# Moving the second direction's chain one step ahead and its products one step back in the heads of a hybrid encoder layer

## The reference, cut to what matters

```python
kf, gf = gates(z_fwd, lb_fwd)
kb, gb = gates(z_bwd, lb_bwd)
o_f = _gla_scan(q, kf, v, gf)
rev = lambda a: jnp.flip(a, axis=1)
o_b = rev(_gla_scan(rev(q), rev(kb), rev(v), rev(gb)))
return o_f + o_b
...
b = jnp.cumsum(gb, axis=-2)
o_inter = jnp.einsum('bhtk,bhkv->bhtv', qb * jnp.exp(b), state)
diff = b[:, :, :, None, :] - b[:, :, None, :, :]
decay = jnp.exp(jnp.where(tri[:, :, None], diff, NEG))
att = jnp.einsum('bhtk,bhsk,bhtsk->bhts', qb, kb, decay)
o_intra = jnp.einsum('bhts,bhsv->bhtv', att, vb)
```

## Time and profile before

| | us |
|---|---|
| median of 3 runs | 1864.23 (1863.73 to 1864.8) |
| profiled execution | 1865.62 |
| its span | 1863.9 |
| TensorE busy | 1803.9 (97% of the span) |
| DVE busy | 1193.5 (64%) |
| ACT busy | 835.3 (45%) |
| GpSimd busy | 197.1 (11%) |
| mean granted TensorE clock | 0.985 |

### The profile page before, as it was taken

How to read it: one execution, slowest core, us unless ns; L and a number is a source line. 1 busy time by engine, 2 the same in 40 slices (tenths; PEclk the granted TensorE clock), 3 DMA queues, 4 the chain that set the end, 5 groups by cost and what they waited for, 6 DMA issues and landing times.

```text
span 1863.9 us, 24074 instructions
## 1 busy us (share of the span) xinstructions
PE 1803.9 (97%) x9337; PEld 1551.5 (83%) x9337; DVE 1193.5 (64%) x1408; ACT 835.3 (45%) x1133; POOL 197.1 (11%) x205
## 2 busy tenths in 40 slices
PE   6999999999999999999999999999999999999998
PEld 5899999888778787878787887878888888888887
DVE  6977776788577778686877767776444432244332
ACT  7444444443556556474747464645322232234221
POOL 4000000000130304040302112220000000000000
PEclk9999999999999999999999999999999999999999
DMA  7343444675523232323233231324545535565332
GB/s 227 92 122 114 149 132 141 198 259 163 161 71 108 84 97 88 102 85 89 82 99 91 74 112 55 110 78 153 174 137 152 157 131 163 167 240 180 127 131 75
DMA packets 287661, 240.89 MB, mean 129 GB/s; under 512 B 9657, under 2 KB 233944, under 8 KB 286032
## 3 DMA queue, kind: packets, MB, share of 16 engines
q1 hardware_dynamic: 284096, 227.59, 39.8%
q0 software_dynamic: 3472, 12.05, 1.8%
HBM read 210.80 MB, written 28.80 MB: 129 GB/s over the span
## 4 chain that ended last, share of the span: by engine, by line
PE 76%; DVE 12%; ACT 7%; issue 3%; DMA 1%; SPq 0%; ACTq 0%; DVEq 0%
PE mm_ps L1869 8%; PE mm_ps L1871 8%; PE mm_ps L1870 8%; PE mm_ps L2094 5%; PE mm_ps L2095 5%; PE mm_ps L2093 5%; DVE dif L1476 3%; PE ax_ps L1938 2%; PE ax_ps L1856 2%; PE ax_ps L1858 2%; PE ax_ps L1857 2%; PE ax_ps L1871 2%; PE ax_ps L1870 2%; PE ax_ps L1869 2%; PE ax_ps L2095 2%
## 5 line engine op out<-in xcount | busy, mean ns | idle before, releaser
L343 DVE TENSOR_TENSOR w_lo<-w_raw,w_hi 128x1024 fp32r<-128x1024 f32 (+1 forms) x200 | 271.6, 1365 | 382.5 <-ACT w_hi L334 382.3
L334 ACT ACTIVATE w_hi<-w_raw 128x1024 fp32r<-128x1024 f32 (+1 forms) x200 | 226.8, 1138 | 427.4 <-PE ax_ps L2095 208.5
L1869 PE MATMUL mm_ps<-act_hl,w_hi 128*128 128x512 f32 x960 | 384.6, 401 | 1.3 <-DVE w_lo L343 1.3
L1871 PE MATMUL mm_ps<-act_hl,w_lo 128*128 128x512 f32 x960 | 374.7, 390 | 0.0
L1870 PE MATMUL mm_ps<-act_hl,w_hi 128*128 128x512 f32 x960 | 374.3, 390 | 0.0
L1871 PEld LDWEIGHTS mm_ps<-act_hl,w_lo 128*128 128x128 f32 x960 | 180.1, 188 | 38.9
L1869 PEld LDWEIGHTS mm_ps<-act_hl,w_hi 128*128 128x128 f32 x960 | 180.6, 188 | 36.8 <-issue 1.7
L1870 PEld LDWEIGHTS mm_ps<-act_hl,w_hi 128*128 128x128 f32 x960 | 180.6, 188 | 35.3
L962 ACT ACTIVATE q_hi<-q_raw 128x1024 fp32r<-128x1024 f32 x84 | 87.6, 1057 | 141.7 <-DVE q_raw L1319 81.2
L2093 PE MATMUL mm_ps<-w_hi,act_hl 128*128 128x512 f32 x384 | 149.9, 390 | 0.0
L2095 PE MATMUL mm_ps<-w_lo,act_hl 128*128 128x512 f32 x384 | 149.4, 389 | 0.0
(11 more groups left out here) (299 smaller groups left out, 3818.5 us busy)
## 6 DMA issues: line engine op xcount, KB each, us to landing
w_raw<-in_w_in SPq DMA_DIRECT2D x120, 512.0 KB, 3.8
q_raw<-in_w_in SPq DMA_DIRECT2D x56, 512.0 KB, 5.8
r_in<-in_w_in SPq DMA_DIRECT2D x56, 512.0 KB, 4.7
w_raw<-in_w_ple_gate SPq DMA_DIRECT2D x20, 768.0 KB, 4.4
w_raw<-in_w_out SPq DMA_DIRECT2D x16, 768.0 KB, 4.3
w_raw<-in_w_branch_a SPq DMA_DIRECT2D x16, 512.0 KB, 3.7
w_raw<-in_w_branch_b SPq DMA_DIRECT2D x16, 512.0 KB, 3.7
g_ab<-gate_dram SPq DMA_DIRECT2D x14, 512.0 KB, 4.2
```

Of the source, the lines that this page charges most:

```text
L334: nc.scalar.activation(w_hi[:, s, 0:width], w_raw[:, s, 0:width], ACT.Copy).then_inc(hi_done, 1)
L343: nc.vector.tensor_tensor(w_lo[:, s, 0:width], w_raw[:, s, 0:width], w_hi[:, s, 0:width].bitcast(F32), ALU.subtract).then_inc(lo_done, 1)
L1869: MM(bank, wh, m_hi[:, k0 + k, :], start=start and k == 0, stop=False)
L1871: mm = MM(bank, wl, m_hi[:, k0 + k, :], start=False, stop=stop and k == kn - 1)
```

## The change

The table of steps puts unit 7 at step 7 instead of 8. The second direction's chain starts at step 8 instead of 9 on ACT and DVE, and goes on at steps 9 and 10 instead of 10 and 11. The first direction's key turning, masks, products and updates move one step ahead with it, with the same neighbours on TensorE. The second direction's products go from step 11 to 12, the last level products from 12 to 13, the second updates and the first mean square from 13 to 14; on DVE the masks of levels 0 and 1 and of the second base products go from 12 to 13, those of levels 2 and 3 and the sum from 13 to 14; on ACT the second key turning goes from 12 to 13. The lists of GpSimd and SP are the same as before. No instruction is added or removed on any engine.

```diff
--- before.py
+++ after.py
@@ -72,7 +72,7 @@
     TA = {j: n + 1 for n, j in enumerate(TILES)}
     NJ, NU = len(TILES), 2 * len(TILES)
     STEPS = 18
-    STEP_UNIT = {i: n for n, i in enumerate(i for i in range(STEPS) if i not in (7, 10, 14, 16))}
+    STEP_UNIT = {i: n for n, i in enumerate(i for i in range(STEPS) if i not in (8, 10, 14, 16))}
     U_MERGE = H * NU
     U_BRANCH = U_MERGE + 8
     U_OUT = U_BRANCH + 2 * KT
@@ -1111,9 +1111,9 @@
                     elif i == 0:
                         act.wait_ge(lb_step, 1)
                         A(lb_col[:, 2, :], lb_col[:, 1, :], ACT.Exp).then_inc(lb_step, 1)
-                    if i == 9:
+                    if i == 8:
                         keys_t(h, 0)
-                    if i == 12:
+                    if i == 13:
                         keys_t(h, 1)
                     if i in (14, 16):
                         root(h, (i - 14) // 2)
@@ -1127,11 +1127,11 @@
                         pre_stored(act)
                     if i % 2 == 0 and i >= 2 and i // 2 - 1 in TILES:
                         tile(h, i // 2 - 1)
-                    if i in (5, 9):
-                        chain(h, i // 9)
-                    if i in (6, 7, 10, 11):
-                        n = 2 if i % 4 == 2 else 4
-                        decays(h, i // 10, n, n + 2)
+                    if i in (5, 8):
+                        chain(h, i // 8)
+                    if i in (6, 7, 9, 10):
+                        n = 2 if i in (6, 9) else 4
+                        decays(h, i // 9, n, n + 2)
 
             head(0)
             for h in range(1, H):
@@ -1630,21 +1630,21 @@
                            ALU.mult).then_inc(low_ready, 1)
                     if i in (4, 6):
                         forget_gate(h, i // 2 - 2)
-                    if i == 9:
+                    if i == 8:
                         base_products(h, 0)
-                    if i == 12:
+                    if i == 13:
                         base_products(h, 1)
-                    if i == 13:
+                    if i == 14:
                         level_products(h, 2)
                         level_products(h, 3)
                         att_total(h)
-                    if i in (5, 9):
-                        chain(h, i // 9)
-                    if i in (6, 7, 10, 11):
-                        chain(h, i // 10, first=2 if i % 4 == 2 else 4)
+                    if i in (5, 8):
+                        chain(h, i // 8)
+                    if i in (6, 7, 9, 10):
+                        chain(h, i // 9, first=2 if i in (6, 9) else 4)
                     if i == 17 and h > 0:
                         dve.wait_ge(zb_stored, 16 * h)
-                    if i == 11:
+                    if i == 10:
                         states(h, 0)
                     if i == 14:
                         states(h, 1)
@@ -2016,18 +2016,18 @@
                         columns(us, u, mm_ps[:, n % 3, :], 8 * (u % 2), 8, u % 2 == 0, u % 2 == 1, act_hi, act_lo)
                     if h > 0:
                         late(i, h - 1)
-                    if i == 8:
+                    if i == 7:
                         intra(h, 0)
-                    if i == 10:
+                    if i == 9:
                         updates(h, 0)
-                    if i == 11:
+                    if i == 12:
                         intra(h, 1)
-                    if i == 12:
+                    if i == 13:
                         pe.wait_ge(q_side, 12 * h + 12)
                         pe.wait_ge(k_side, 12 * h + 12)
                         pe.wait_ge(att_part[1], h + 1)
                         levels(2).then_inc(lev_done, 1)
-                    if i == 13:
+                    if i == 14:
                         updates(h, 1)
                         pe.wait_ge(mean_ready, 1)
                         pe.wait_ge(base_part, 2 * h + 2)
```

## The result

The changed kernel takes 1832.78 us (median of 4, 1832.41 to 1833.87) against 1864.05 (1863.73 to 1864.8) for the kernel before in the same comparison: a ratio of 0.9833, 95% interval 0.9816 to 0.985, or 31.3 us faster. The profiled execution took 1832.41 with a span of 1830.7, 33.2 us less than the 1865.62 of the profiled execution before. The prediction said 1830, with a range of 1812 to 1852.

What follows compares the result with a forecast made beforehand. TensorE was taken to bound the heads, with one wait for DVE's queries and its clock loss. Per head 7.18 - 2.1 - 0.75 = 4.33, 34.2 us over eight heads less 0.4, gave 1830 us, range 1812 to 1852.

Steps and rivals of the forecast that it cites:

- The stall: TensorE between units 9 and 10, waiting for DVE's scaled queries, then at half clock: 7.18 us per head to win.
- The split of unit 10: DVE's split of unit 10's weights, now behind the scan and fourth distance: new TensorE wait of 2.1 us per head.
- the meeting: DVE's fourth distance beside GpSimd's product on the first level: 0.55 us extra ahead of unit 10's split.
- The second meeting: By the lock rule read strictly, GpSimd could also hit unit 10's split: wait about 2.6, gain 4 us smaller.
- The clock in the new wait: TensorE's clock before unit 10: expected to hold at a wait of 2.1 us; at 3.1 it may not.
- The tail: End of a head: later masks of levels 2 and 3 delay the states, output products 0.75 us per head late.
- The small leads: Unit 11's split ready 0.1 to 0.2 us ahead, the next head's unit 1 split 0.7; no cost counted.
- the first rival: Clock falls in the new wait before unit 10 too: gain 1.56 us per head, 1852 us; chance 0.14.
- the second: Rival: no wait before unit 10, only the tail paid: 6.43 us per head, 1813 us; chance 0.14.
- the equal stall: Rival: one stall traded for an equal one, wait near 3.7 us with clock lost, within 0.2%; chance 0.04.
- the slower one: Rival: unit 10's split so late that TensorE waits 4.6 us with clock lost: 1871 us; chance 0.06.

Runs made afterwards that it cites:

- the added matmuls: Kernel before, with 16 matmuls of constants added into a free bank ahead of the old wait in each head: 1845.35 us, 0.9894.
- the version with no new price: Kernel before, with only TensorE's second-direction products, last level products, second updates and ACT's second key turning a step later; DVE's list unchanged: 1810.55 us, 0.9716.
- The experiment with the chain alone: Changed kernel with the second direction's products, masks, updates and key turning set back to their old steps, the chain still sooner: 1849.41 us, 0.9916.

## Why the prediction was right, step by step

The head is 4.33 us shorter (99.08 to 94.75), and 4.33 was forecast. The mechanism and the places of the waits came as forecast; that the number agrees to the hundredth is luck, since three terms were off by 0.16 to 0.31 each and cancel:

| term, us per head | predicted | measured (third head) |
|---|---|---|
| stall and clock won | 7.18 | 7.18 (the wait gone, clock 1.00; slower products in the fourth row) |
| wait of unit 10 for its split, by starts | -2.1 | -1.79 |
| output products behind the late states | -0.75 | -0.91 |
| other level and base products | 0 | -0.19 |
| sum | 4.33 | 4.29 (pitch: 4.33) |

**The stall.** 10.01 us where 2.83 would do was right in both parts. That the second part is the clock, was shown by the added matmuls. The queries were ready in time in every version that put unit 10 first, and the version with no new price gave 7.12 per head.

**The split of unit 10.** The mechanism was right: the first customer moved, and the split stood behind the start of the chain. The scan starts 4.04 behind unit 7's end (703.01 to 707.05) where it was 5.41 (712.56 to 717.97), so 1.37 earlier and not 0.97. The 0.40 is a sum of small ones: unit 9's split was through 0.15 sooner than my 713.9 has it (704.20, which is 713.75 on the old scale), and z_b, the two level products and the copy took 1.00, 1.22 and 0.63 by their starts, where 717.0 leaves them 1.0, 1.4 and 0.7. From the scan to the end of the split I had 10.45, and it is 10.46 (707.05 to 717.51), with the meeting of 0.54 for which I took 0.55. Unit 10 then started 0.14 behind the split, for which I had 0.05. By the Trainium skill's rule of the lock (SBUF — State Buffer, "SBUF: two separate sides") one of the two engines is held back until the other's instruction is through. The trace agrees in this row as well: the distance ends at 716.37, 0.55 after GpSimd's product. The second meeting, in the split itself, did not come: it took 1.22 for my 1.2.

**The clock in the new wait.** It held, with 1.62 us idle. My reason was the 2.9 us at which it fell before. The experiment with the chain alone shows that the reason was weaker than I thought: at 3.33 it held in two heads and fell in the others, so where it fell in one trace does not say where it falls in the next.

**The tail.** States at 740.14 plus 0.97; the output products 6.77 behind unit 12's start (734.57 to 741.34) against 5.93 before (749.35 to 755.28), 0.84 for my 0.75, and 0.07 more in the products themselves. The experiment that moved the masks back gave 7.5 us, and 0.90 per head by the distance of the heads.

**The small leads.** Unit 11's split (taken as half of the pair at 723.30) ended about 1.1 before TensorE asked, and I had 0.1 to 0.2. DVE's list behind the fourth distance took about 8.6 to there and not my 9.5, so this was less close than forecast. The next head's unit 1 met no wait. But the tail's delay on DVE did reach TensorE once, behind the last head, where the merge's work is added to DVE's list:

```profile
1241.64 0.44 PE L1994 MATMUL ax_ps<-ident,prob 128*128 128x128 f32 x2 [0.44 <-DVE prob L1598]
```

From the last head's output products to the first branch product (mm_ps<-za_hi, line 1869) it took 56.34 before (1250.32 to 1306.66) and takes 57.50 now (1215.07 to 1272.57). With the masks moved back it takes 56.34 again (1209.25 to 1265.59), so this loss of 1.16 is the masks' too; the prediction's sum had no term for it. The whole of the 33.2 then reads: 34.35 won from the first unit (470.85, now 469.95) to the last head's output products, 1.16 lost here, 0.90 won ahead of the first head and 0.89 lost behind the first branch product. The last two lie outside the change, and their cause is open. The start of the first head lies between 469.95 and 471.31 in the eight traces, though no engine's list ahead of it differs.

**Rivals.** No stretch at the lower clock, so the first rival is out; the wait before unit 10 is there, so the second; and the equal stall and the slower one would have needed a wait twice as long, with the clock lost. What the prediction did not ask is whether both halves of the change were wanted. It had the numbers for it, since it found the queries ready (729.8) before unit 10's end (731.0) with no other effect. The experiments show that the earlier chain, which puts unit 10's split behind the scan, costs 1.79 a head at unit 10. Leaving out only the chain's move gains 0.75 a head net (94.0 for 94.75), since the masks of levels 0 and 1 then cost 0.9.

## What to carry to other kernels

When a wait is covered by putting a big block of work in front of it, move only the waiting engine's list first: here that (with ACT's turning of the keys, which follows TensorE) gave 54 us, and moving the producers and the masks too gave 22 of them back. For each block put forward, look up when its own inputs are made: before the change unit 10's split was through 18 us ahead of its use (717.43 for 735.42), and after it that split was the last to arrive. And look for masks or sums that can go into an idle gap of their engine before they are put behind something that waits.

## What the runs showed of the hardware

- TensorE's clock (one execution each): idle for 1.62 us (1.50 in the first head) it stayed at 1.00 in every head; idle for 3.86 to 4.27 it fell in every head; idle for 3.33 the eight level products behind took 2.05 us in two of seven heads and 2.67 to 3.78 in the other five, and 3.27 behind the 3.21 of the first head. Sixteen spare matmuls in the gap of 4.4 made the kernel 19 us faster.
- A distance on DVE (a subtraction of two operands in SBUF) next to a product on GpSimd took 1.22 instead of 0.68, and two weight splits next to the bias sums on GpSimd (722.98 to 727.18 in the changed kernel) 3.23 instead of 2.34. How long a block on DVE takes depends on what GpSimd is doing when it comes, so a move on DVE changes durations as well as places.
